# An earlier ScalarE table load, and a new place for GpSimd's pooling and one product, in a four-layer transformer forward pass

## The reference, cut to what matters

```python
proj = h @ w_in
(dn_qkv, dn_z, dn_b, dn_a, ret_q, ret_k, ret_v, ret_g, pool_u, gates) = jnp.split(proj, ...)
qkv = jax.nn.silu(causal_depthwise_conv(dn_qkv, dn_conv))     # 4 taps
q, k, v = l2_normalize(q), l2_normalize(k), v                 # 4 heads of 128
o_dn = gated_delta_rule(q, k, v, beta, g)    # chunks of 64, (I + M)^-1 by levels, then a scan over 4 chunks
o_pool = multiscale_pool(pool_u, ...)        # trailing means of 2, 4, 8, 16 frames, minus the frame, a 128x128 map a group
o_ret = chunkwise_retention(rotary(ret_q), rotary(ret_k), ret_v, log_gamma)
y = gate0 * (o_dn @ w_branch_dn) + gate1 * (o_pool @ w_branch_pool) + gate2 * (o_ret @ w_branch_ret)
return y @ w_out
```

## Time and profile before

| what | value |
|---|---|
| median of three runs | 1844.22 us (1843.95 to 1845.06) |
| the profiled execution, its own time | 1844.57 us |
| its span, first to last instruction | 1842.8 us, mean granted TensorE clock 0.998 |
| TensorE busy | 1807.2 us, 98% |
| VectorE busy | 1248.1 us, 68% |
| ScalarE busy | 952.8 us, 52% |
| GpSimd busy | 307.2 us, 17% |

### The profile page before, as it was taken

How to read it: one execution, slowest core, us unless ns; L and a number is a source line. 1 busy time by engine, 2 the same in 40 slices (tenths; PEclk the granted TensorE clock), 3 DMA queues, 4 the chain that set the end, 5 groups by cost and what they waited for, 6 DMA issues and landing times.

```text
span 1842.8 us, 37206 instructions
## 1 busy us (share of the span) xinstructions
PE 1807.2 (98%) x15880; PEld 1717.0 (93%) x15880; DVE 1248.1 (68%) x1668; ACT 952.8 (52%) x1377; POOL 307.2 (17%) x174
## 2 busy tenths in 40 slices
PE   7999999999999999999999999999999999999998
PEld 7889998998888999999989999999999899999998
DVE  6895677665689547777658775587647784677643
ACT  5634466544554345564445445556534445556533
POOL 0050221000002303200002353320001352321000
PEclk9999999999999999999999999999999999999999
DMA  6453354656445333655565563456665663455663
GB/s 242 153 164 108 126 172 156 208 190 208 151 152 174 119 115 138 206 179 181 193 212 174 188 191 127 138 178 200 199 193 174 222 197 126 140 168 195 195 196 102
DMA packets 91524, 315.54 MB, mean 171 GB/s; under 512 B 11616, under 2 KB 12768, under 8 KB 91104
## 3 DMA queue, kind: packets, MB, share of 16 engines
q1 hardware_dynamic: 90784, 312.60, 52.6%
q10 hardware_dynamic: 576, 0.57, 0.1%
HBM read 302.90 MB, written 1.05 MB: 165 GB/s over the span
## 4 chain that ended last, share of the span: by engine, by line
PE 83%; DVE 12%; ACT 3%; issue 1%; DMA 0%; SPq 0%; DVEq 0%; ACTq 0%
PE bank L2019 81%; DVE wlo L1143 4%; DVE area L1143 3%; DVE area L1149 2%; ACT area L646 1%; ACT whi L652 1%; PE bank L2601 1%; DVE hl L1149 1%; DVE xT L1149 1%; DVE area L1663 1%; DVE area L1661 0%; DMA raw<-in_weights 0%; ACT L634 0%; DVE area L1146 0%; PE bank L2622 0%
## 5 line engine op out<-in xcount | busy, mean ns | idle before, releaser
L1143 DVE TENSOR_TENSOR wlo<-raw,whi 128x1024 fp32r<-128x1024 f32 x514 | 659.2, 1298 | 390.5 <-ACT whi L652 390.2
L2019 PE MATMUL bank<-hh,whi 128*128 128x256 f32 x2896 | 817.2, 283 | 20.2 <-DVE wlo L1143 17.4
L2019 PE MATMUL bank<-hh,wlo 128*128 128x256 f32 x2906 | 800.8, 277 | 0.0
L2019 PE MATMUL bank<-hl,whi 128*128 128x256 f32 x2896 | 793.0, 277 | 0.0
L652 ACT CAST whi<-raw 128x1024 fp32r<-128x1024 f32 x568 | 585.2, 1047 | 369.3 <-PE bank L2019 327.2
L2019 PEld LDWEIGHTS bank<-hh,whi 128*128 128x128 f32 x2896 | 545.4, 188 | 36.6 <-DVE wlo L1143 20.7
L2019 PEld LDWEIGHTS bank<-hh,wlo 128*128 128x128 f32 x2906 | 546.4, 188 | 0.0
L2019 PEld LDWEIGHTS bank<-hl,whi 128*128 128x128 f32 x2896 | 540.8, 188 | 1.5 <-issue 1.4
L1799 POOL TENSOR_TENSOR area<-area 128x512 f32<-128x512 f32 (+4 forms) x84 | 133.4, 1595 | 538.4 <-ACT area L646 213.1
L1799 POOL TENSOR_TENSOR wlo<-raw,whi 128x1024 fp32r<-128x1024 f32 x54 | 134.6, 2494 | 392.7 <-ACT whi L652 392.7
L2019 PE MATMUL bank<-FH,whi 128*128 128x256 f32 x640 | 177.4, 277 | 0.0
(11 more groups left out here) (132 smaller groups left out, 1903.3 us busy)
## 6 DMA issues: line engine op xcount, KB each, us to landing
raw<-in_weights SPq DMA_DIRECT2D x568, 512.0 KB, 4.0
area<-area SPq DMA_DIRECT2D x100, 64.0 KB, 3.7
area<-area SPq DMA_DIRECT2D x16, 128.0 KB, 3.9
cst<-in_const SPq DMA_DIRECT2D x1, 1188.0 KB, 8.3
cst<-in_const SPq DMA_DIRECT2D x1, 1024.5 KB, 5.9
xT<-in_x SPq DMA_DIRECT2D x4, 256.0 KB, 7.3
out<-xT SPq DMA_DIRECT2D x4, 256.0 KB, 2.8
area<-in_lev SPq DMA_DIRECT2D x2, 384.0 KB, 7.1
```

The source lines that it names most:

```text
L1143: return v.tensor_tensor(dst, x, y, op)
L2019: return e.matmul(ps, x, y, start=start, stop=stop, skip_group_check=skip)
```

## The change

Three edits. On ScalarE, the set that holds Silu is loaded by name ahead of `rest(qkv)`. In `mixers`, which all engines share, a step of `pooling` goes behind the steps of `delta` with index 14 and higher, not 7 and higher. On GpSimd, the product Aq * EG with its two waits moves from behind level 0 to behind level 3.

```diff
+SILU = "silu_and_others"
...
     for i, n in enumerate(delta):
         yield n
-        if i > 6:
+        if i > 13:
             next(pooling, None)
...
                 next(qkv)
                 next(qkv)
                 next(dn)
+                tables(SILU)
                 rest(qkv)
...
                 yield 1
-                g.wait_ge(*e_dn.at("KQ", L, 1))
-
-                g.wait_ge(*v_dn.at("Y", L, 0))
-                tt(Aq[:, :], Aq[:, :], EG[:, :], OP.mult).then_inc(*g_dn.up("q", L))
                 yield 1
                 for s in range(1, 6):
                     yield 1
                     yield 1
+                    if s == 3:
+                        g.wait_ge(*e_dn.at("KQ", L, 1))
+                        g.wait_ge(*v_dn.at("Y", L, 0))
+                        tt(Aq[:, :], Aq[:, :], EG[:, :], OP.mult).then_inc(*g_dn.up("q", L))
```

## The result

The changed kernel took 1847.72 us (median of 20 executions, 1845.42 to 1850.63), the kernel before 1844.35 us beside it (20 executions, 1842.54 to 1847.45). The ratio is 1.0017, with a 95% interval of 1.0011 to 1.0022: about 3.1 us slower, 2.0 to 4.1. That is under 0.2%, so "no change that can be told" holds as the forecast bounded it, but the sign is clear and the time lies above the range of 1842.4 to 1847.2. The profiled execution took 1847.30 us with a span of 1845.5, 2.7 us more than before. Its lines stand one or two further down in the file (L647, L653, L1145, L1151, L1801, L2021).

A forecast was written before the change was run, and what follows sets the result against it. TensorE bounds the kernel, with idle gaps released by VectorE. Table load -2.56, sum 1 +2.22, sum 0 +1.11 and product 0 make +0.77 us on the median of 1844.22: 1845.0 us, range (8 in 10) 1842.4 to 1847.2.

The forecast's parts named there:

- Part 1: ScalarE's table load in qkv moves into idle time, shortening TensorE's gap there: -1.28 us a layer, -2.56 in two.
- rival 4: Table load in qkv gains nothing, through a late cast or a second load: +3.33 us, 1847.6 us, chance 0.06.
- Part 2: GpSimd's new order ahead of T0 of level 1: +2.22, +1.11 and 0 us; the rest off the path.
- the meetings: GpSimd operations locking out VectorE work on two SBUF inputs ahead of T0: +1.11 us for each sum that meets.
- sum 1: Second GpSimd sum of rotated(0), ahead of the product: certainly delays T0 in both layers, +2.22 us.
- sum 0: First GpSimd sum of rotated(0): a coin toss, delays T0 in one of two layers, +1.11 us (0 to +2.22).
- the product: GpSimd's Aq*EG keeps its start behind Y and still stretches VectorE's residual ahead of T0: 0 us change.
- rival 3: Sums do not meet VectorE: -2.56 us, 1841.7 us; 1839.6 if the product also leaves the stretch; chance 0.12.
- the clock: TensorE's granted clock behind the T0 gap: number of falls to half clock kept as before, 0 us in the sum.
- a fall: TensorE's drop to the 1.2 GHz level behind the T0 gap: one costs 1.51 us.
- rival 2: Late pooling's last subtraction stalls TensorE in level 4: up to 1.61 us a layer, +3.99 in all, 1848.2 us, chance 0.14.
- second clock fall: TensorE's clock also falls behind T0's gap in layer 1: +2.28 us in all, 1846.5 us, chance 0.26.

The follow-up runs named there:

- experiment 9: Kernel before with pooling from chunk 7 behind T0, last subtraction and product behind VB, old table load place: 2.4 us faster than the kernel before.
- experiment 10: Kernel before with the new table load, pooling from chunk 7 behind T0, last subtraction and product behind VB, run again: 5.7 us faster than the kernel before.
- experiment 4: Changed kernel with GpSimd's sums of chunk pair 0, and so the product, waiting for T0 of level 1: 5.5 us faster than the kernel before.
- experiment 6: Kernel before with the new table load, pooling from chunk 7 behind T0, last subtraction and product behind VB: 7.0 us faster than the kernel before.
- experiment 1: Kernel before with only the table load moved two chunk casts sooner: 1.5 us faster than the kernel before (-3.3 to +0.4).
- experiment 3: Changed kernel with the product back behind level 0, ahead of the sums, pooling still late: 0.2 us faster than the kernel before (-2.2 to +1.7).
- experiment 2: Changed kernel without the table load edit, so the GpSimd part alone: 5.4 us slower than the kernel before.
- experiment 7: Changed kernel with pooling's last subtraction behind a wait for VB of the last chunk pair: 3.0 us slower than the kernel before.
- experiment 8: Changed kernel with the product waiting for T0 of level 1 in place of Y: 1.3 us slower than the kernel before (-0.4 to +3.0).
- experiment 5: Changed kernel with pooling from chunk 7 as before, so table load and moved product only: 14.6 us slower than the kernel before.

## Why the prediction was wrong

**Part 1, right, a little small.** Forecast -1.28 a layer, measured -1.41 and -1.42 in the gaps and -2.8 us in experiments 9 and 10. What was missed is the overlap between taps and Silu. The Trainium skill (ScalarE: Activation LUTs, "What ACT_TABLE_LOAD costs") would have added a drain of 1380 ns; the cast behind the load starts 0.01 us after it, so this trace shows none, and rival 4 is out.

**Part 2, the meetings: right.** Forecast +2.22 for sum 1, +1.11 for sum 0 in one of two layers, 0 for the product; measured +2.88 in all. That sum 0 met in just one layer is the coin toss coming out as its mean, which is luck. The price of these meetings is about 1.0 us, not 1.11. The table gives it as a line. With no meeting ahead of T0, idle is 1.47 to 1.56 (experiments 4, 6, 9, 10); one, 2.50 to 2.57 (before, experiments 1 and 3); two, 3.44 to 3.57 (changed layer 1, experiments 2, 7 and 8); three, 4.53 to 4.55. Each adds 0.9 to 1.1; experiment 5, where one meeting cost 2.20, lies off the line. That an operation of GpSimd and one of VectorE with two SBUF inputs don't run together, as the Trainium skill states (SBUF — State Buffer, "SBUF: two separate sides"), agrees with every meeting read here; rival 3 is out.

**The step that failed: the clock.** "I keep the number of falls as it is in the forecast and give the other as a rival." The argument that the longer gap makes a fall more likely was right, and the forecast set it aside: the sum has 0 for this term. In the profiled execution it was +1.86 us: a longer fall in layer 0 and a new one in layer 1. By the timed executions it is no accident: 16 of 20 of the changed kernel and 6 of 80 of the kernel before have a mean granted clock of 0.996 or less, and with T0 idle near 1.55 (experiments 4, 6, 9 and 10) 34 of 35 show 0.999. The price of a fall (1.51) was right (1.36 in layer 1); its chance (0.26) was far too small. No experiment holds the gap and changes the clock alone, so the worth of this term rests on the stretches of the traces.

**And rival 2 came in beside it.** Pooling's last subtraction stretched the residual ahead of VB in both layers (to 2.22 and 2.23 us) and cost 0.68 us in layer 1, of the 1.61 at most. In layer 0 it ended at 136.86 and cost 0.01, where the forecast had put 1.0 on an end at 136.7: the longer gap and the half clock had held TensorE back by 1.1 us (119.76 against 118.66), and the point from which the subtraction decides had moved with it. That last is read from the times of both and was not tried by itself. The wait was put down to the subtraction by experiment 7, its worth in time only by the trace.

**How the numbers followed.** The rivals were treated as if they shut each other out, but nothing keeps the second clock fall and the level-4 wait from coming in together, and on top of the forecast's own meetings, which had made the longer gap. The forecast's +0.77, its price of one more fall (1.51) and the 0.68 measured in level 4 make +2.96, 0.1 under the ratio's 3.1. So close a match is partly luck: load and meetings came out 0.27 and 0.45 us below the forecast, the clock 0.35 above one fall's price. On the median of 1844.22 that is 1847.2 us, the very end of the range, which had been drawn as if no two of them could come in together.

## What to carry to other kernels

An operation that waits may be the gate for all that stands behind it in its queue: before it is moved, look for what then starts early (40 us earlier in experiment 5), not only for what the operation itself will meet. Where GpSimd and VectorE both use operands in SBUF, count the meetings ahead of each due time of TensorE; keeping all of them behind T0 and VB made this kernel 2.4 us faster with the old load, and 5.7 and 7.0 us with the new one. Where a gap of the bounding engine grows, add the clock's answer to the forecast instead of holding it apart as a rival: in these traces the half clock came behind none of the 8 T0 gaps of 1.47 to 1.56 us, behind 4 of the 6 of 2.50 to 2.57, and behind 9 of the 10 of 3.44 us and more.

## What had not been expected of the hardware

Two further sources of spread can be tied to none of the edits. The matmuls of one stage can run at another pitch while the granted clock reads 1.00. In both traces below, of experiments 9 and 10, the same 46 steps of 128x256 matmuls lie between the second row and the third, in the gated MLP of layer 1: 845.99 - 840.57 = 5.42 us, 117.8 ns each, against 843.25 - 838.02 = 5.23, 113.7 ns each.

```profile
840.35 0.38 PE L2022 MATMUL bank<-hh,whi 128*128 128x256 f32 x1 [0.95 <-DVE wlo L1144]
840.57 0.28 PE L2022 MATMUL bank<-hl,whi 128*128 128x256 f32 x1
...
845.99 0.28 PE L2022 MATMUL bank<-hh,wlo 128*128 128x256 f32 x1
...
973.51 0.49 PE L2022 MATMUL bank<-area 128*128 128x128 f32 x2 [0.17 <-DVE area L1214]
```

```profile
837.80 0.39 PE L2023 MATMUL bank<-hh,whi 128*128 128x256 f32 x1 [0.94 <-DVE wlo L1145]
838.02 0.28 PE L2023 MATMUL bank<-hl,whi 128*128 128x256 f32 x1
...
843.25 0.28 PE L2023 MATMUL bank<-hh,wlo 128*128 128x256 f32 x1
...
968.63 0.60 PE L2023 MATMUL bank<-area 128*128 128x128 f32 x3 [0.17 <-DVE area L1215]
```

From the first row to the idle time ahead of the last the stretch takes 132.99 us in the one and 130.66 in the other, 2.33 us apart, with no gap over 0.3 us behind the first row. Only the 128x256 matmuls are slower: the 128x512 ones that follow them, from about 910 us, have a pitch of 228.9 ns in both. The traces of experiments 5 and 7 have the slow form too. In experiment 7 the first microseconds were also slow: TensorE reached its gap in qkv 1.8 us later than the changed kernel did. Together these make its profiled span 3.2 us longer than the changed kernel's though its waits are shorter, and they are why single executions here are read by their gaps and not by their spans. What sets the pitch stays open.

The clock did not fall behind every long gap: behind 3.47 us in layer 0 of experiment 2 the trace shows the full level, and behind 2.50 in layer 1 of experiment 1 the half one. Between gap and fall these runs show a likelihood and not a fixed limit.
